# Attention units between projection groups, 128-row token transposes and a split output projection in an encoder block

## The chip, the cores and the metric

The kernel runs on one core of one Trainium2 chip. The metric is the device time of one launch in microseconds (us), lower is better. A core has TensorE (PE; its weight loads are listed apart as PEld), VectorE (DVE), ScalarE (ACT), GpSimd (POOL) and SyncE (SP), which run their own instruction streams and wait for each other on semaphores; 16 DMA engines move data.

## What is computed

One layer of a bidirectional encoder on a prompt of 1024 tokens and a sample of 512, all in float32, 1024 channels. The core of the reference:

```python
xn = rmsnorm(x, norm1_g[l])
proj = xn @ w_in[l]                       # q, k, v: 3 groups x 4 heads x 64 each; u: 768
for g, (win, dil) in enumerate(GROUPS):   # ((128, 1), (512, 4), (2048, 16))
    o, lse = dilated_group(q[:, :, g], k[:, :, g], v[:, :, g], ..., dil, (win // 2) // dil)
...
att = jnp.sum(wts[..., None] * jnp.stack(outs, axis=0), axis=0)
four = fourier_mix(u)
gates = jax.nn.sigmoid((xn @ w_gate[l] + b_gate[l]).astype(jnp.float32))
...
mix = gates[:, :, 0] * (att @ w_attn_br[l]) + gates[:, :, 1] * (four @ w_four_br[l])
x = x + mix @ w_out[l]
x = x + expert_choice(rmsnorm(x, norm2_g[l]), w_router[l], w_exp_gate[l], w_exp_up[l], w_exp_down[l])
```

Each query of a head group sees 64 keys to either side in its residue class of the dilation (1, 4 or 16). The expert choice picks, for each of 16 experts, the 128 prompt tokens and 64 sample tokens with the highest router weight, and runs a SwiGLU with 2048 inner channels on them.

## The kernel before

Matrix products of float32 values are mostly done as three products of the fast float32r type: an operand is split into a rounded high part (ACT copies it) and a low part (DVE subtracts), and high x high, high x low and low x high are summed in PSUM. Products that aren't split run as plain float32. The program is a chain of blocks with a barrier between; in a block each engine has an order written by hand.

**Norm.** RMSNorm, transposes of the tokens to xhigh and xlow, and the bias tables. Ends near 67 us.

**Projections and attention** (lines 466 to 775). For each head group g, `project(g)` on PE makes q and k with 12 groups of 24 matmuls of 512 columns (lines 603 to 605), then v with 12 groups of 24 matmuls of 256 columns (lines 572 to 574). PSUM banks 6 and 7 take turns; ACT copies q out, DVE k and v. The values go through DRAM to be put in order by residue class: SP stores the 12 token tiles (`vrows<-vst`, 8 slots), waits until all are stored, and loads 12 to 16 tiles `V` (`class_rows`). Then come the 12 attention units of the group, a unit being 128 queries of one class with its 4 heads: `scores(n)` on PE (line 623), `biased(n)` on DVE (line 722: adds the bias, takes the maximum), `exps(n)` on ACT (line 678), `turn(n)` on PE (transposes, line 639), `turned(n)` on ACT and DVE (copies to pT), `outputs(n)` on PE (line 655) and the copy to `orow` on DVE (line 743). PE's order is scores(n), turn(n-2), outputs(n-3). After the third group, `channels()` makes u: 36 groups of 24 matmuls of 256 columns. Weight block n of w_in lies in one of two buffers, is loaded when block n-2 is done, and cut in two by `high_block` (ACT, 2048 columns) and `low_block` (DVE).

Units come in three kinds. Of the 36, 16 have one piece of 128 keys (the sample of group 1, all of group 2); 20 have two pieces. Of those, 8 have two pieces of 128 keys, and 12 one of 128 and one of 64 (all 8 prompt units of group 1, and the first and last of each sequence in group 0, where the residue class begins or ends).

**Fourier mixing and merge**, then **gates** (three-part products); not touched.

**Router** (from 1267 us). For each of 12 token tiles PE runs `out(t)` (line 1185): mix @ w_out as 16 plain float32 matmuls of 512 columns, then `turn` (line 1195: 8 transposes), `logits` (1205) and `turn_aff` (1212) of earlier tiles. DVE adds the residual, norms and makes the softmax. Once the 8 prompt tiles have their logits, DVE also searches the top 128 of 1024 tokens in 16 rounds (`top(0, r)`), and after the last tile the top 64 of 512 in 8 rounds. SP loads the first expert's units 0, 1 and 2 of weights (2 MB each) into `raw` at the start of this block.

**Experts** (from 1518 us, lines 1389 to 1600). A loop over 16 experts. POOL gathers the chosen rows (`xg`), PE transposes them in `turn_tokens` (lines 1446 and 1447: 8 times 128 rows of the prompt and 64 rows of the sample, by turns), ACT and DVE split them, and PE runs `gate_up` and `down` while ACT and DVE split the streamed weights. `turn_tokens(e + 1)` stands behind the second of eight steps of `down(e)`.

```python
                for g in range(NG):
                    project(g)
                    a, b = first_unit[g], first_unit[g + 1]
                    for n in range(a, b + 3):
                        if n < b:
                            scores(n)
                        if a <= n - 2 < b:
                            turn(n - 2)
                        if a <= n - 3:
                            outputs(n - 3)
                channels()
```

## Time and profile before

| | us |
|---|---|
| median of 3 runs | 3399.98 |
| the three runs | 3392.88, 3399.98, 3400.17 |
| profiled execution | 3397.87 |
| its span in the trace | 3395.8 |
| busy in the span: PE / PEld | 3189.2 / 2761.7 |
| busy: DVE / ACT / POOL | 1855.9 / 1435.8 / 119.2 |

The span is the time from the first to the last instruction of the profiled execution; the rest lies around it. The granted clock is TensorE's: 1.00 is 2.4 GHz, 0.50 is 1.2 GHz. A matmul's duration in a row is longer than its share of a stream, since matmuls overlap; what one costs in a stream is the distance between starts.

### The profile page before, as it was taken

The numbers are of one execution on the slowest core, as the hardware profiler recorded it, in microseconds if no ns is written. First come the engines' busy times: TensorE is split into PE (matmuls) and PEld (weight loads), VectorE is DVE, ScalarE is ACT, GpSimd is POOL, SyncE is SP. The second block draws the span as 40 slices with busy tenths as digits, with TensorE's granted clock in tenths as the row PEclk, the third lists the DMA queues.
The fourth block names the chain that finished last, engine by engine and source line by source line (L and its number), as shares of the span: only waits on it lengthen the run. The fifth ranks groups of instructions, "written<-read, shape, count | busy, mean of one in ns | idle before, by whom it ended". The sixth has DMA issues, their size and how long they took to land. (4 is left out here: it accounts for less than half of the span.)

```text
span 3395.8 us, 45550 instructions
## 1 busy us (share of the span) xinstructions
PE 3189.2 (94%) x17512; PEld 2761.7 (81%) x17512; DVE 1855.9 (55%) x2764; ACT 1435.8 (42%) x1969; POOL 119.2 (4%) x133
## 2 busy tenths in 40 slices
PE   5989898999999999949999999999999999999993
PEld 4878787974778774529999999999999999999993
DVE  4141313042443422486777777777777777767773
ACT  4030312121432322225555655565556555655552
POOL 0000000000000000000000000000000000000000
PEclk9989696999999999969999999999999999999997
DMA  4111111031233334226766777677667766777664
GB/s 165 41 57 39 55 35 63 17 102 44 77 91 95 110 118 167 75 81 210 238 229 233 249 238 228 229 247 238 228 234 249 237 228 235 248 231 228 234 229 164
DMA packets 468127, 553.25 MB, mean 163 GB/s; under 512 B 14379, under 2 KB 384043, under 8 KB 467916
## 3 DMA queue, kind: packets, MB, share of 16 engines
q1 hardware_dynamic: 460876, 526.94, 45.8%
q0 software_dynamic: 7168, 25.17, 3.3%
q8 instruction: 56, 0.92, 0.1%
q14 instruction: 27, 0.22, 0.0%
HBM read 507.87 MB, written 44.19 MB: 163 GB/s over the span
## 5 line engine op out<-in xcount | busy, mean ns | idle before, releaser
L1462 PE MATMUL ps<-xsplit,wh 128*128 128x384 f32 x4096 | 1167.8, 359 | 2.2 <-DVE xsplit L1557 2.2
L1464 PE MATMUL ps<-xsplit,wl 128*128 128x192 f32 x4096 | 1026.2, 251 | 0.0
L1550 DVE TENSOR_TENSOR wl<-raw,wh 128x2048 fp32r<-128x2048 f32 x384 | 876.9, 2284 | 115.0 <-ACT wh L1507 113.9
L1507 ACT ACTIVATE wh<-raw 128x2048 fp32r<-128x2048 f32 x384 | 734.5, 1914 | 347.5 <-PE ps L1486 321.7
L1464 PEld LDWEIGHTS ps<-xsplit,wl 128*128 128x128 f32 x4096 | 783.3, 191 | 0.6
L1462 PEld LDWEIGHTS ps<-xsplit,wh 128*128 128x128 f32 x4096 | 769.6, 188 | 3.0 <-issue 2.4
L1521 ACT ACTIVATE low<-ps 128x384 f32<-128x384 f32 x256 | 126.0, 492 | 433.4 <-PE ps L1464 433.4
L1566 DVE TENSOR_TENSOR gu<-ps,low 128x384 f32<-128x384 f32 x256 | 142.8, 558 | 219.9 <-ACT low L1521 219.9
L1079 DVE TENSOR_TENSOR glow<-graw,ghigh 128x1024 fp32r<-128x1024 f32 x72 | 88.1, 1225 | 237.3 <-ACT ghigh L1035 237.3
L1481 PE MATMUL ps<-wh,hsplit 128*128 128x512 f32 x512 | 201.9, 394 | 0.0
L1483 PE MATMUL ps<-wl,hsplit 128*128 128x512 f32 x512 | 200.4, 391 | 0.0
L1485 PE MATMUL ps<-wh,hsplit 128*128 128x512 f32 x512 | 200.4, 391 | 0.0
L1486 PE MATMUL ps<-wl,hsplit 128*128 128x512 f32 x512 | 200.1, 391 | 0.0
L1482 PE MATMUL ps<-wh,hsplit 128*128 128x512 f32 x512 | 200.1, 391 | 0.0
L1035 ACT ACTIVATE ghigh<-graw 128x1024 fp32r<-128x1024 f32 x72 | 76.4, 1061 | 213.4 <-DMA graw<-in_w_gate_dram 138.8
L572 PE MATMUL ps<-whigh,xhigh 128*128 128x256 f32 x576 | 164.3, 285 | 2.0 <-ACT u L709 1.4
L1020 PE MATMUL ps<-xh,ghigh 128*128 128x512 f32 x384 | 152.6, 397 | 13.1 <-DVE xlow L1086 13.1
L573 PE MATMUL ps<-wlow,xhigh 128*128 128x256 f32 x576 | 164.0, 285 | 0.0
L574 PE MATMUL ps<-whigh,xlow 128*128 128x256 f32 x576 | 163.9, 285 | 0.0
L1021 PE MATMUL ps<-xlow,ghigh 128*128 128x512 f32 x384 | 152.0, 396 | 0.0
L1022 PE MATMUL ps<-xh,glow 128*128 128x512 f32 x384 | 151.8, 395 | 0.0
L678 ACT ACTIVATE sc<-sc,negm 128x128 f32<-128x128 f32 (+2 forms) x144 | 61.9, 432 | 171.1 <-DVE negm L728 171.1
(205 smaller groups left out, 4484.6 us busy)
## 6 DMA issues: line engine op xcount, KB each, us to landing
raw<-in_w_exp_gate_dram SPq DMA_DIRECT2D x128, 1024.0 KB, 5.2
raw<-in_w_exp_up_dram SPq DMA_DIRECT2D x128, 1024.0 KB, 7.4
raw<-in_w_exp_down_dram SPq DMA_DIRECT2D x128, 1024.0 KB, 6.1
graw<-in_w_gate_dram SPq DMA_DIRECT2D x96, 256.0 KB, 2.8
wraw<-in_w_in_dram SPq DMA_DIRECT2D x12, 1024.0 KB, 5.2
graw<-in_w_four_br_dram SPq DMA_DIRECT2D x24, 384.0 KB, 3.5
xin<-in_x_dram SPq DMA_DIRECT2D x12, 512.0 KB, 3.7
xres<-in_x_dram SPq DMA_DIRECT2D x12, 512.0 KB, 3.5
```

Source lines behind the costliest of these rows:

```text
L572: pe.matmul(bank, high[k], whigh[:, n % 2, k, :], start=k == 0, stop=False)
L573: pe.matmul(bank, high[k], wlow[:, n % 2, k, :], start=False, stop=False)
L574: mm = pe.matmul(bank, low[k], whigh[:, n % 2, k, :], start=False, stop=k == KT - 1)
L1462: pe.matmul(ps[:, bank, 0:2 * CAP], wh[:, q % AHEAD, tile], xsplit[:, k, :, :].rearrange("p s t -> p (s t)"), start=k == 0, stop=False)
L1464: mm = pe.matmul(ps[:, bank, CAP:2 * CAP], wl[:, q % AHEAD, tile], xsplit[:, k, 0, :], start=False, stop=k == KT - 1)
L1481: pe.matmul(prompt, hsplit[:, k, H_LOW], wh[:, q % AHEAD, cols], start=first, stop=False)
L1482: pe.matmul(prompt, hsplit[:, k, H_HIGH], wh[:, q % AHEAD, cols], start=False, stop=False)
L1483: pe.matmul(prompt, hsplit[:, k, H_HIGH], wl[:, q % AHEAD, cols], start=False, stop=end)
L1485: pe.matmul(sample, hsplit[:, k, H_SAMPLE], wh[:, q % AHEAD, cols], start=first, stop=False)
L1486: mm = pe.matmul(sample, hsplit[:, k, H_SAMPLE], wl[:, q % AHEAD, cols], start=False, stop=end)
L1507: act.activation(cut_part(wh, q), raw_part(q), ACT.Copy).then_inc(w_high, 1)
L1550: dve.tensor_tensor(cut_part(wl, q), raw_part(q), cut_part(wh, q).bitcast(F32), ALU.subtract).then_inc(w_cut, 1)
```

## The change

Four things.

1. **Order of projections and attention.** The two sequences get their own q, k and V tiles (P for prompt, S for sample). Groups of matmuls run in the order v, q, k of the prompt, then v, q, k of the sample, for each head group, then u. The units of one part (head group, sequence) run during the groups of the next part: behind a group of matmuls PE runs outputs(n-2), turn(n-1), scores(n). A part of 8 units meets 8 groups (4 of v, 2 of q, 2 of k) and starts one unit behind each; a part of 4 units starts one behind every second group. Scores have 2 PSUM banks in place of 4, sc 2 buffers in place of 3. The weight blocks are now 18 of the same 256 columns for q, k and v (9 before), each loaded for either sequence, and 3 for u.
2. **Values.** Stores of v tiles and loads of V are issued by POOL in place of SP, with 3 slots in place of 8, and each part's loads stand between its own v and q groups.
3. **Output projection.** `out(t)` runs 48 float32r matmuls (lines 1239 to 1241 of the changed kernel) in place of 16 plain float32. ACT and DVE first split w_out (16 pieces of 128x512 each) and then each tile of the mix, one tile ahead. The split copy of w_out lies where `raw` units 1 and 2 were, so these are loaded behind the last output projection.
4. **Token transposes.** xgS has 128 rows, the last 64 set to zero once by POOL ahead of the first gather; both transposes of a pair now have 128 rows and columns.

PE behind a group of values, in the attention of head group 0, prompt (kT and kP are keys, V and vP values, sc the scores). Before:

```order
L623 MATMUL ps<-kT,qT 128x256 x4
L639 MATMUL ps<-ident,sc 128x128 x8
L655 MATMUL ps<-V,pT 128x64 x8
L623 MATMUL ps<-kT,qT 128x256 x4
L639 MATMUL ps<-ident,sc 128x128 x8
```

Now, at the end of the sample's fourth v group and the start of its first q group (L642 to L644 are v, L628 to L630 are q):

```order
L642 MATMUL ps<-whigh,xhigh 128x256
L643 MATMUL ps<-wlow,xhigh 128x256
L644 MATMUL ps<-whigh,xlow 128x256
L689 MATMUL ps<-vP,pT 128x64 x8
L674 MATMUL ps<-ident,sc 128x128 x8
L658 MATMUL ps<-kP,qP 128x256 x4
L628 MATMUL ps<-xhigh,whigh 128x512
L629 MATMUL ps<-xlow,whigh 128x512
```

The units stood back to back; now 24 matmuls of a projection stand between two of them.

DVE at the start of the router block. Before, behind the last mix of the gates:

```order
L1270 TENSOR_TENSOR xres<-xres,ps 128x512 x2
L1274 TENSOR_SCALAR stat<-stat 128x1
L1276 RECIPROCAL stat<-stat 128x1
```

Now:

```order
L1336 TENSOR_TENSOR xlow<-mix_93,xlow 128x8x128
L1343 TENSOR_TENSOR flow<-fourT,wo_h 128x512 x6
L1343 TENSOR_TENSOR alow<-attT,wo_h 128x512 x2
L1343 TENSOR_TENSOR flow<-fourT,wo_h 128x512 x6
L1343 TENSOR_TENSOR alow<-attT,wo_h 128x512 x2
L1336 TENSOR_TENSOR xlow<-mix_93,xlow 128x8x128
L1355 TENSOR_TENSOR xres<-xres,ps 128x512 x2
```

DVE's first residual add now stands behind one split of the mix, 16 of w_out and the next of the mix.

The diff, cut to its core:

```diff
-        qT = at("qT", 128, [P, 2, TOKENS])
-        kT = at("kT", 140, [P, 2, TOKENS])
-        V = at("V", 152, [P, MAXV, GW])
-        band = at("band", 168, [P, 2 * HEADS, 2 * P])
-        same = at("same", 176, [P, 2, HEADS, P])
-        sc = at("sc", 180, [P, 3, HEADS, 2 * P])
+        VSLOTS = 3
+        qT = [at("qP", 128, [P, 2, SEQS[0][1]]), at("qS", 164, [P, 2, SEQS[1][1]])]
+        kT = [at("kP", 136, [P, 2, SEQS[0][1]]), at("kS", 168, [P, 2, SEQS[1][1]])]
+        V = [at("vP", 144, [P, MAXV[0], GW]), at("vS", 172, [P, MAXV[1], GW])]
+        band = at("band", 156, [P, 2 * HEADS, 2 * P])
+        same = at("same", 177, [P, 2, HEADS, P])
+        sc = at("sc", 181, [P, 2, HEADS, 2 * P])
+        vst = at("vst", 189, [P, VSLOTS, GW])
...
+        wo_h = at("wo_h", 96, [P, KT, D], F32R)
...
-        xg = [at("xgP", 88, [CAPS[0], D]), at("xgS", 92, [CAPS[1], D])]
-        raw = [at(f"raw{i}", kb, [P, 16, WB]) for i, kb in enumerate((96, 112, 176, 128))]
+        xg = [at("xgP", 88, [P, D]), at("xgS", 92, [P, D])]
+        raw = [at(f"raw{i}", kb, [P, 16, WB]) for i, kb in enumerate((176, 96, 112, 128))]
...
+        for g in range(NG):
+            for s, (base, size) in enumerate(SEQS):
+                first = len(groups)
+                for kind in "vqk":
+                    n = len(block_groups)
+                    block_groups.append([])
+                    for i in range(size // P if kind == "v" else 2 * size // CH):
+                        block_groups[n].append(len(groups))
+                        groups.append(Group(kind, n, g, s, i % 2 if kind != "v" else i, i // 2))
+                phases.append((first, len(groups)))
...
+        starts = [[] for _ in groups]
+        n = 0
+        for (g, s), (first, end) in zip([(g, s) for g in range(NG) for s in range(2)], phases[1:]):
+            count = sum((x[0], x[2].s) == (g, s) for x in units)
+            for j in range(count):
+                starts[first + j * min(2, (end - first) // count)].append(n)
+                n += 1
...
+        def cut_after(n):
+
+            return block_groups[n - 1][min(1, len(block_groups[n - 1]) - 1) if len(block_groups[n - 1]) > 2 else 0]
+
+        cut_at = {cut_after(n): n for n in range(2, NB)}
...
+            @block.gpsimd
+            def _(pool):
+                def class_rows(g, s):
+                    base, size = SEQS[s]
+                    if g:
+                        pool.wait_ge(o_ev, units_before(g - 1, s))
+                    rows_of = vrows[base:base + size, :]
+                    first = sum(x[0] < s for x in PLANS[g][1])
+                    for v, (_, r, classes, a) in enumerate([x for x in PLANS[g][1] if x[0] == s]):
+                        rows = rows_of.rearrange("(n r) f -> r n f", r=GROUPS[g][1] // classes)
+                        pool.dma_start(v_tile(s, g, first + v), rows[r, a:a + P, :]).then_inc(v_ld, 16)
+
+                for p, x in enumerate(groups):
+                    if x.kind != "v":
+                        continue
+                    if x.i == 0 and x.n:
+                        pool.wait_ge(v_ld, v_loads(*((x.g, 0) if x.s else (x.g - 1, 1))))
+                    slot, before = v_slot(p)
+                    pool.wait_ge(*evacuated(p))
+                    row = SEQS[x.s][0] + x.i * P
+                    pool.dma_start(vrows[row:row + P, :], vst[:, slot, :]).then_inc(v_st[slot], 16)
+                    if p == block_groups[x.n][-1]:
+                        for q in block_groups[x.n][-VSLOTS:]:
+                            slot, before = v_slot(q)
+                            pool.wait_ge(v_st[slot], 16 * (before + 1))
+                        class_rows(x.g, x.s)
...
-                for g in range(NG):
-                    project(g)
-                    a, b = first_unit[g], first_unit[g + 1]
-                    for n in range(a, b + 3):
-                        if n < b:
-                            scores(n)
-                        if a <= n - 2 < b:
-                            turn(n - 2)
-                        if a <= n - 3:
-                            outputs(n - 3)
-                channels()
+                for p, x in enumerate(groups):
+                    project(p, x)
+                    for n in starts[p]:
+                        if n >= 2:
+                            outputs(n - 2)
+                        if n >= 1:
+                            turn(n - 1)
+                        scores(n)
+                outputs(NU - 2)
+                turn(NU - 1)
+                outputs(NU - 1)
...
+                dve.wait_ge(t_out, 16)
+                for p, x in enumerate(groups):
+                    if p:
+                        for n in starts[p - 1]:
+                            if n == 0:
+                                dve.wait_ge(t_tab, 16 * 3)
                             biased(n)
-                        if a <= n - 2 < b:
-                            turned(n - 2)
-                        if a <= n - 3:
-                            outputs(n - 3)
-                        if n == a + 2:
-                            low_block(dve, 3 * g + 4)
-                low_block(dve, 11)
+                    if x.kind in "kv":
+                        evacuate(p, x)
+                    if p in cut_at:
+                        low_block(dve, cut_at[p])
+                    for n in starts[p]:
+                        if n >= 2:
+                            outputs(n - 2)
+                        if n >= 1:
+                            turned(n - 1)
+                outputs(NU - 2)
+                turned(NU - 1)
+                outputs(NU - 1)
...
+                sp.wait_ge(r_y, 2 * NT)
+                for j in (1, 2):
+                    load_unit(sp, 0, j)
...
+                    high, low = mix_part(t, 0), mix_part(t, 1)
                     for nb in range(2):
+                        bank, cols = ps[:, 6 * (t % 2) + nb, :], slice(nb * CH, (nb + 1) * CH)
                         for k in range(KT):
-                            mm = pe.matmul(ps[:, 6 * (t % 2) + nb, :], mix_of(t // 4)[:, k, (t % 4) * P:(t % 4 + 1) * P],
-                                           w_out_at(k)[:, nb * CH:(nb + 1) * CH], start=k == 0, stop=k == KT - 1)
+                            if t == 0:
+                                pe.wait_ge(wo_cut, nb * KT + k + 1)
+                            pe.matmul(bank, high[:, k, :], wo_h[:, k, cols], start=k == 0, stop=False)
+                            pe.matmul(bank, high[:, k, :], w_out_low(k)[:, cols], start=False, stop=False)
+                            mm = pe.matmul(bank, low[:, k, :], wo_h[:, k, cols], start=False, stop=k == KT - 1)
                         mm.then_inc(r_y, 1)
...
+                high_mix(0)
+                high_w_out()
...
+                def low_mix(t):
+                    dve.wait_ge(mix_high, t + 1)
+                    dve.tensor_tensor(mix_part(t, 1), mix_tile(t), mix_part(t, 0).bitcast(F32), ALU.subtract).then_inc(mix_cut, 1)
+
+                def low_w_out():
+                    for nb in range(2):
+                        for k in range(KT):
+                            cols = slice(nb * CH, (nb + 1) * CH)
+                            dve.wait_ge(wo_high, nb * KT + k + 1)
+                            dve.tensor_tensor(w_out_low(k)[:, cols], w_out_at(k)[:, cols], wo_h[:, k, cols].bitcast(F32),
+                                              ALU.subtract).then_inc(wo_cut, 1)
+
+                low_mix(0)
+                low_w_out()
...
+                pool.memset(xg[1][CAPS[1]:P, :], 0.0).then_inc(x_zero, 1)
+                pool.wait_ge(x_zero, 1)
...
-                        at_col = (k % 2) * CAP
-                        pe.transpose(ps[:, k // 2, at_col:at_col + CAPS[0]], xg[0][:, k * P:(k + 1) * P], ident[:, :])
-                        mm = pe.transpose(ps[:, k // 2, at_col + CAPS[0]:at_col + CAP], xg[1][:, k * P:(k + 1) * P],
-                                          ident[0:CAPS[1], 0:CAPS[1]])
+                        at_col = (k % 2) * 2 * P
+                        pe.transpose(ps[:, k // 2, at_col:at_col + P], xg[0][:, k * P:(k + 1) * P], ident[:, :])
+                        mm = pe.transpose(ps[:, k // 2, at_col + P:at_col + 2 * P], xg[1][:, k * P:(k + 1) * P], ident[:, :])
```

## Rows read from the trace of the kernel before

**Rows 1.** Windows: length; busy (count) of PE, PEld, DVE, ACT, POOL; clock; DMA; GB/s.

```profile
69.50:704.30 634.80, 593.79 (x3552) 531.24 (x3552) 133.98 (x502) 124.52 (x395) 0.00 (x0) 0.87 0.14 44
173.00:242.20 69.20, 56.92 (x384) 48.40 (x384) 34.22 (x147) 31.99 (x111) 0.00 (x0) 0.83 0.21 66
344.50:432.40 87.90, 76.81 (x336) 63.60 (x336) 30.78 (x149) 28.67 (x113) 0.00 (x0) 0.60 0.18 55
535.40:596.30 60.90, 46.68 (x240) 42.42 (x240) 25.73 (x145) 25.05 (x109) 0.00 (x0) 0.54 0.22 70
1267.30:1420.40 153.10, 147.74 (x489) 77.86 (x490) 36.93 (x84) 36.96 (x65) 0.00 (x0) 0.98 0.41 144
1420.40:1518.00 97.60, 59.68 (x201) 34.10 (x200) 88.97 (x158) 14.96 (x30) 0.17 (x2) 0.74 0.10 38
```

**Rows 2.** Timeline of PE, projections: start us, us, engine, line, operation, count.

```profile
86.54 0.39 PE L605 MATMUL ps<-xhigh,wlow 128*128 128x512 f32 x1
...
137.76 0.28 PE L572 MATMUL ps<-whigh,xhigh 128*128 128x256 f32 x1
...
157.08 0.28 PE L574 MATMUL ps<-whigh,xlow 128*128 128x256 f32 x1
```

**Rows 3.** Timeline of PE, two units of head group 0.

```profile
221.82 1.90 PE L655 MATMUL ps<-V,pT 128*128 128x64 f32 x16
223.65 1.13 PE L623 MATMUL ps<-kT,qT 64*128 64x256 f32 x8
225.22 1.03 PE L639 MATMUL ps<-ident,sc 128*64 128x128 f32 x8 [0.44 <-issue]
226.09 2.76 PE L655 MATMUL ps<-V,pT 128*128 128x64 f32 x15
...
228.81 0.49 PE L623 MATMUL ps<-kT,qT 64*128 64x192 f32 x3
```

**Rows 4.** Timeline of PE, head group 2, scores of two following units.

```profile
568.75 1.33 PE L623 MATMUL ps<-kT,qT 64*128 64x128 f32 x8
...
572.65 0.61 PE L623 MATMUL ps<-kT,qT 64*128 64x128 f32 x2
```

**Rows 5.** A window inside the attention of head group 0.

```profile
205.00:240.00 35.00, 33.45 (x271) 29.81 (x269) 20.51 (x91) 18.52 (x66) 0.00 (x0) 1.00 0.09 33
```

**Rows 6.** Timeline of PE, first matmuls behind two gaps.

```profile
185.68 1.94 PE L639 MATMUL ps<-ident,sc 128*128 128x128 f32 x8 [6.05 <-DVE pT L509]
...
857.94 0.77 PE L1020 MATMUL ps<-xh,ghigh 128*128 128x512 f32 x1 [4.60 <-DVE xlow L1086]
```

**Rows 7.** Timeline of the first unit: DVE's first bias, PE's first transposes.

```profile
174.13 0.36 DVE L722 CUSTOM_DVE_ANT_0 sc<-ps,band 128x192 f32<-128x192 f32 x1 [1.19 <-PE ps L623]
...
177.49 1.07 PE L639 MATMUL ps<-ident,sc 128*64 128x128 f32 x8 [0.97 <-ACT sc L678]
```

**Rows 8.** Timeline of PE, one row of the router block.

```profile
1377.90 5.31 PE L1185 MATMUL ps<-fourT,xnT 128*128 128x512 f32 x12
...
1391.64 1.04 PE L1195 MATMUL ps<-ident,xn 128*128 128x128 f32 x8
...
1394.33 1.88 PE L1185 MATMUL ps<-fourT,xnT 128*128 128x512 f32 x4
```

**Rows 9.** Groups by line and form: busy us, mean ns, idle before.

```profile
L1086 DVE TENSOR_TENSOR xlow<-xnT,xh 128x1024 fp32r<-128x1024 f32 x12 | 13.9, 1219 | 0.0
```

**Rows 10.** Timeline of PE, token transposes of an expert in the loop.

```profile
1620.71 0.33 PE L1446 MATMUL ps<-ident,xgP 128*128 128x128 f32 x1
...
1621.17 0.33 PE L1446 MATMUL ps<-ident,xgP 128*128 128x128 f32 x1
```

**Rows 11.** The page's costliest group.

```profile
L1462 PE MATMUL ps<-xsplit,wh 128*128 128x384 f32 x4096 | 1167.8, 359 | 2.2 <-DVE xsplit L1557 2.2
```

**Rows 12.** Timeline of POOL and PE at the start of the experts.

```profile
1520.48 2.38 POOL L1419 DMA_INDIRECT xgS<-normed,idx_inS  x1 [0.30 <-issue]
...
1528.10 0.48 PE L1446 MATMUL ps<-ident,xgP 128*128 128x128 f32 x1 [11.16 <-DMA xgS<-normed,idx_inS]
```

More of the change, by code:

```diff
@@ L475, in encoder @@
         v_st, v_ld = sems("v_st", VSLOTS), sem("v_ld")
[L477 to L483 removed]
         units = [(g, i, t) for g in range(NG) for i, t in enumerate(PLANS[g][0])]
[L486 to L487 removed]
+        NU = len(units)
@@ L489, in encoder @@
         u_tiles = [(s, par, j) for s, (_, n) in enumerate(SEQS) for par in range(2) for j in range(n // 2 // P)]
-        first_unit = [next(n for n, v in enumerate(units) if v[0] == g) for g in range(NG)] + [len(units)]
-        NU = len(units)
+        Group = namedtuple("Group", "kind n g s i c")
+        groups, block_groups, phases = [], [], []
+        for g in range(NG):
[8 more added lines that the diff above has]
+                phases.append((first, len(groups)))
@@ new lines, in encoder @@
+        for m in range(3):
+            n = len(block_groups)
+            block_groups.append(list(range(len(groups), len(groups) + NT)))
+            groups += [Group("u", n, None, None, i, m) for i in range(NT)]
+        phases.append((block_groups[-3][0], len(groups)))
+        NB = len(block_groups)
+        starts = [[] for _ in groups]
[5 more added lines that the diff above has]
+                n += 1
@@ new lines, in evacuated, with units_before, v_loads @@
+        def evacuated(p):
+            kinds = {"q": "q", "k": "kv", "v": "kv", "u": "u"}
+            kind = kinds[groups[p].kind]
+            return {"q": q_ev, "kv": kv_ev, "u": u_ev}[kind], sum(kinds[x.kind] == kind for x in groups[:p + 1])
+        def units_before(g, s):
+            return sum((u[0], u[2].s) <= (g, s) for u in units)
+        def v_loads(g, s):
+            return 16 * sum(1 for h in range(NG) for v in PLANS[h][1] if (h, v[0]) <= (g, s))
+        v_groups = [p for p, x in enumerate(groups) if x.kind == "v"]
@@ L616, in scores @@
                 def scores(n):
                     g, i, t = units[n]
-                    if n >= 2:
-                        pe.wait_ge(s_max, 4 * (n - 1))
+                    if n == 0 or units[n - 1][0] != g or units[n - 1][2].s != t.s:
+                        for kind, sem_ in (("q", q_ev), ("k", kv_ev)):
+                            last = max(p for p, x in enumerate(groups) if (x.kind, x.g, x.s) == (kind, g, t.s))
+                            pe.wait_ge(sem_, evacuated(last)[1])
+                    if n:
+                        pe.wait_ge(s_max, 4 * n)
@@ L711, in _ @@
+                for p, x in enumerate(groups):
+                    if p:
+                        for n in starts[p - 1]:
+                            exps(n)
+                    if x.kind in "qu":
+                        evacuate(p, x)
+                    if p in cut_at:
+                        high_block(act, cut_at[p])
+                    for n in starts[p]:
+                        if n >= 1:
+                            turned(n - 1)
+                turned(NU - 1)
             @block.vector
```

277 lines of the change are left out of this document (121 added, 156 removed).

## The prediction

> **What bounds the kernel now.** I read the page first: PE is busy for nearly all of the span, in the expert loop without a break (its costliest group waited 2.2 us in all [rows 11]). So time can be won only where PE waits, where it runs at half clock, or where its own work shrinks. Next the windows by stage [rows 1]. Projections and attention take 634.8 us at a mean granted clock of 0.87. The loss lies in the three attention stretches of 69.2, 87.9 and 60.9 us, at clocks of 0.83, 0.60 and 0.54: PE looks busy there, but much of it at 1.2 GHz. In the router PE is busy for 147.7 of the first 153.1 us, then DVE takes over with 89.0 of 97.6 us.
>
> Then the timeline of PE, to see why the clock falls. PE stands still for 6 us until the values have come back from DRAM and the turned scores can be copied [rows 6], and the attention behind that gap runs at half pace. In head group 0 it recovers: for 35 us units run at 1.00 with PE busy for 33.45 us [rows 5]. In groups 1 and 2 it hardly does.
>
> **1. Projections and attention.** I build the new stage as a sum of PE's work at full clock, since every other engine has less to do.
>
> Projections: 864 matmuls of 512 columns. From 86.54 to 137.76 us 226 of them start, so one costs 0.227 us: 195.8 us. Then 1728 of 256 columns; 161 start between 137.76 and 157.08 us, 0.120 each: 207.4 us [rows 2]. Splitting by sequence changes no count. Together 403.2 us.
>
> Units: two pieces of 128 keys: outputs 1.83 (221.82 to 223.65), scores 1.13 (to 225.22, less 0.44 idle), transposes 0.87 (to 226.09), 3.83 us. With a 64-key piece the outputs take 2.72 (226.09 to 228.81), so 4.72 us [rows 3]. With one piece I have only the half-clock row: 3.90 us from scores to scores [rows 4], so 1.95 us at full clock. Sum: 8 x 3.83 + 12 x 4.72 + 16 x 1.95 = 118.5 us.
>
> Is the new order fed? The tightest steps are v groups with a unit behind each (12 of them, 4 in each sample part). PE's work in one is 24 x 0.120 = 2.88 us plus the unit, 6.7 us for two full pieces. Beside it runs the chain from scores(n) to turn(n). The first unit shows it: DVE's first bias at 174.13, PE's transposes at 177.49, 3.4 us for 192 keys [rows 7]. I add 1.2 us for the scores ahead of the bias (DVE's wait in that row), an estimated 0.6 us for 256 keys in place of 192 and 0.9 us for the transposes themselves: 6.1 us. It just fits. One-piece units have 4.8 us of PE work, and a chain shorter in proportion. Behind q and k groups (24 x 0.227 = 5.4 us more) there is room. In each sample part's v block, DVE has a weight cut in the same queue ahead of the orow and pT copies and the next bias, so the next bias comes some 2 us late; PE then waits 1.5 us, three times: 4.5 us. Elsewhere cuts hide behind q and k groups. Small gaps: rows 3 shows one of 0.44 us; between 0 and 0.44 x 36 = 16 us, I take 4, since the projection group in between absorbs most. The first matmuls still run slow, 3 us as before. At the end outputs(34), turn(35) and outputs(35) stand behind the last u group, and the block can't end before the last copy and store: 3 us more than the short tail now. Sum: 403.2 + 118.5 + 4.5 + 4 + 3 + 3 = 536.2 us against 634.8. **Gain 98.6 us**, bounds 85 and 112. Where it comes from: about 45 us of standing still, the rest clock.
>
> Values: the stall of 6 us goes because the loads of a part now have its q and k groups as cover (8 x 5.4 = 43 us in a prompt part). Now POOL issues them. No row shows a plain DMA from POOL; its dearest indirect one takes 2.38 us [rows 12], so 12 loads take 29 us at most, under the cover. For stores, 3 slots give 3 x 2.88 = 8.6 us from copy to reuse in the first part, against some 2.4 us to issue and a few to land. I cost it at nothing. SP's attrows stores now stand among weight loads; three orow buffers cover that.
>
> **2. Token transposes.** A pair in the loop costs 1621.17 - 1620.71 = 0.46 us, 3.68 us for 8 [rows 10]. Eight transposes of 128 rows in one shape take 1.04 us as a row, ending beside the next start [rows 8]; less the overlap of the last, 0.11 us each. So 16 equal ones take 1.76 us: 1.92 us less. PE never waits in the loop [rows 11], so all of it counts: 15 x 1.92 = 28.8 us, and about 1.9 us for the first expert. The sample's now move 128 columns where 64 were moved. Upper bound of the cost: a second one as dear as the first, 0.26 us (0.46 less the other's 0.20), so 4.2 us and a loss of 0.5 us each; I take the equal-shape row since it is the same form of instruction. **Gain 30.7 us**, bounds -8 and 31.
>
> Here the Trainium skill speaks against the change: "TensorE: Matmul & The Clock Gate", section "Why this matters for your kernels", says that a small-K matmul takes the same time as a full one. By that rule no time hides in the 64-row shape, and more columns can only add. The trace says otherwise for a mix: 0.23 us on average against 0.11.
>
> **3. Output projection.** A row of the router takes 1394.33 - 1377.90 = 16.43 us, of it 13.74 for 16 plain products, 0.86 each; 48 split ones take 48 x 0.227 = 10.9 us [rows 2, 8]. That is 2.86 us less per tile. For tiles 2 to 8 PE sets the pace, 7 x 2.86 = 20.0 us; DVE is busy for 36.9 of 153 us there [rows 1], so one more split per tile, 1.22 us [rows 9], hides. Tiles 0 and 1 win 5.7 us but PE starts late: one split of the mix on ACT and on DVE (1024 columns, 1.22 us on DVE [rows 9], a little less on ACT) and the first piece of w_out (512 columns, half of that) go first. By my estimate PE starts some 3.1 us later than now, and has then stood still for 5 us. Behind a gap of 4.60 us its matmuls take 0.77 us for 0.39 [rows 6, 2], which costs another 3 us. DVE's 16 pieces, at 0.61 us or a little more each, keep up with PE's 3 x 0.227 = 0.68. Net 0.4 us lost. From tile 9 on DVE sets the end, with two more splits in its queue (tiles 10 and 11): 2.4 us. **Gain 17.2 us**, bounds 8 and 24. The 4 MB of weights that are now loaded behind the last product have over 40 us of top-k search as cover.
>
> **4. The memset** of 64x1024 on POOL stands ahead of the first gather, for which PE waits 11.16 us [rows 12]. Between nothing and twice a DVE pass over 1024 columns (1.22 us [rows 9]); I take 1.2 us lost.
>
> **Sum.** 98.6 + 30.7 + 17.2 - 1.2 = 145.3 us off the profiled execution of 3397.87 us, which lies 2.1 us below the median. From the median 3399.98: **3255 us**.
>
> **Rivals.**
> *Half clock in the tight steps.* The bubbles and transposes of the twelve v steps let the clock drop there. For it: attention ran long stretches at 0.5 with PE busy. Against: rows 5, and in each step now some 3 us of the dense matmuls behind which the clock recovered each time. All twelve (6.7, 7.6 and 4.8 us in the three parts) cost 4 x 19.1 = 76 us more: 3331; half of them 3293. The same page of the Trainium skill, "Part 4: PE-mode transpose", says that transposes don't count as work for the clock; this speaks for the rival, rows 5 against it.
> *Transposes as dear as now.* Only the row count matters, not the mix: the 30.7 us go, up to 8 more are lost: 3286 to 3294.
> *POOL's queue throttles values.* If a store takes over 8.6 us from copy to landing, v groups wait for slots. At 12 us each dense group takes 4 instead of 2.88; over the 24 prompt groups that is 27 us: 3282. The Trainium skill, "SBUF — State Buffer", section "SBUF: two separate sides", says that a POOL-issued DMA takes about 3.1 us in place of 0.62 while a DVE copy of two-port kind holds the shared port; that alone would stay under 8.6 us.
> *Slower than before.* The clock stays at 0.5 through the interleaved stretch, as it did for most of head groups 1 and 2, with PE busy [rows 1]. From the end of the first part PE has 466 us of work at full clock; a share s of it at half clock adds 466 x s, which eats all 145 us from s = 0.31. At s = 0.5 it is 3488.
> *The order doesn't bite:* units wait on their chain as now, at full clock. Then each of 12 tight steps loses some 3 us: 3291.
>
> **How the numbers follow.** Forecast 0.58 (3233 to 3275); half clock in tight steps 0.13; transposes 0.11; POOL 0.06; chain 0.05; persistent half clock 0.04; the rest on the fast side 0.03. The range 3233 to 3305 holds the forecast, most of the transpose, POOL and chain cases and the lighter half of the first rival, some 0.83. What a measurement can tell from no change is about 0.2% (7 us); only the persistent half clock reaches that: faster 0.95, same 0.01, slower 0.04.
>
> **What would show it.** In the changed profile: clock near 1.00 from 76 us to the end of u; that stage 536 us long; no gap of PE over 2 us inside; pairs of token transposes at 0.22 us; router rows at 13.6 us and DVE still last there; POOL's stores spaced by the v groups, not by themselves. A stage over 560 us, or windows at 0.5 in the v blocks, would show the first step wrong; a pair at 0.46 us or more the second.

## The result, and where the 131.7 us went

| | before | changed |
|---|---|---|
| median, us | 3399.8 | 3264.9 (3262.0 to 3265.9) |
| ratio to before, 95% interval | | 0.9606 (0.959 to 0.962) |
| span of the profiled execution, us | 3395.8 | 3264.1 |

The forecast was 3255 us, its range 3233 to 3305. The sum by stage comes from the first matmul of each stage. First the timeline of PE before (start, us, line, what; in brackets the idle time ahead), then after:

```profile
711.21 6.73 PE L814 MATMUL ps<-tabS,u 128*128 128x256 f32 x16 [7.03 <-DMA chan_sb<-c_chan_dram]
1267.41 2.81 PE L1185 MATMUL ps<-fourT,mix 128*128 128x512 f32 x6 [1.85 <-PEq L975]
...
3343.51 0.39 PE L1486 MATMUL ps<-wl,hsplit 128*128 128x512 f32 x1
```

```profile
630.15 5.53 PE L850 MATMUL ps<-tabS,u 128*128 128x256 f32 x16 [8.77 <-DMA chan_sb<-c_chan_dram]
1187.43 0.77 PE L1239 MATMUL ps<-wo_h,xlow 128*128 128x512 f32 x1 [4.89 <-DVE flow L1343]
1430.79 0.45 PE L1535 MATMUL ps<-ident,xgP 128*128 128x128 f32 x1 [13.85 <-DMA xgS<-normed,idx_inS]
3212.12 0.39 PE L1574 MATMUL ps<-wl,hsplit 128*128 128x512 f32 x1
```

With 1528.10 us for the first token transposes of before [rows 12]:

| stage | before | after | change | forecast |
|---|---|---|---|---|
| to the first Fourier matmul | 711.21 | 630.15 | -81.1 | -98.6 |
| from there to the first output projection | 556.20 | 557.28 | +1.1 | (+3.1, start of the split) |
| from there to the first token transposes | 260.69 | 243.36 | -17.3 | -19.1 |
| from there to the last matmul | 1815.41 | 1781.33 | -34.1 | -30.7 |
| tail | 52.3 | 52.0 | -0.3 | 0 |

The forecast of rows 2 and 3 together is -17.2 for the projection and +1.2 for the memset, -16.0; they gave -16.2, of which 2.0 belong to Fourier mixing and gates (557.28 less 3.04 of later start, against 556.20), so the two terms themselves gave -14.2. The windows of the changed kernel (length; busy and count of PE, PEld, DVE, ACT, POOL; clock; DMA; GB/s) answer [rows 1]:

```profile
69.40:621.40 552.00, 549.42 (x3552) 489.44 (x3552) 154.03 (x510) 143.92 (x404) 42.42 (x78) 0.99 0.20 67
180.00:300.00 120.00, 120.00 (x752) 104.18 (x751) 41.67 (x122) 32.78 (x84) 11.88 (x22) 1.00 0.23 76
300.00:470.00 170.00, 168.86 (x992) 145.13 (x991) 55.08 (x197) 46.03 (x141) 14.06 (x26) 0.96 0.21 69
470.00:621.40 151.40, 150.82 (x1148) 143.27 (x1146) 28.24 (x116) 40.60 (x123) 2.17 (x4) 1.00 0.13 42
```

The stage of projections and attention took 634.8 us with 593.8 busy at 0.87. Now it takes 552.0 with 549.4 busy at 0.99. Both halves of the reasoning are seen: PE doesn't wait, and it isn't slow. Still the stage is 16 us longer than the 536.2 of the forecast. The unit rows show why. One-piece unit of head group 2, followed by the first matmul of a group; then outputs, transposes and scores of a unit of head group 1 with pieces of 128 and 64 keys:

```profile
501.02 1.00 PE L689 MATMUL ps<-vP,pT 128*128 128x64 f32 x8
501.85 0.61 PE L674 MATMUL ps<-ident,sc 128*128 128x128 f32 x4
502.39 1.32 PE L658 MATMUL ps<-kP,qP 64*128 64x128 f32 x8
503.64 0.39 PE L642 MATMUL ps<-whigh,xhigh 128*128 128x256 f32 x1
...
311.89 2.87 PE L689 MATMUL ps<-vP,pT 128*128 128x64 f32 x16
314.69 1.07 PE L674 MATMUL ps<-ident,sc 128*64 128x128 f32 x8
315.69 1.75 PE L658 MATMUL ps<-kP,qP 64*128 64x192 f32 x8
317.36 0.50 PE L628 MATMUL ps<-xhigh,whigh 128*128 128x512 f32 x1
```

The unit takes 503.64 - 501.02 = 2.62 us where the sum had 1.95. Outputs and transposes did get short with the clock, 0.83 and 0.54 us. The scores did not: 1.25 us from 502.39 to 503.64 at full clock. Before, at half clock, they took as much, from the row of 568.75 [rows 4] to this row of the kernel before:

```profile
570.01 1.11 PE L639 MATMUL ps<-ident,sc 128*128 128x128 f32 x4
```

That is 1.26 us. So the scores don't scale with the clock here. The scores of head groups 1 and 2 read every 4th or 8th column of qT and kT (`class_cols`); those of head group 0 read neighbouring ones. That became the main question for the chip.

POOL, whose price for a plain DMA no row of before showed, was cheap (line, form, count; busy us, mean ns; idle before):

```profile
L608 POOL DMA_DIRECT2D vrows<-vst x36 | 19.7, 548 | 403.7 <-DVE vst L789 403.7
```

A plain DMA takes POOL 0.55 us to issue, and DVE never waits for a slot: ahead of its copies to vst it waits for PE alone. Now the router and the experts, tile to tile and transpose to transpose:

```profile
1240.22 0.47 PE L1239 MATMUL ps<-wo_h,xlow 128*128 128x512 f32 x1
...
1253.84 0.48 PE L1239 MATMUL ps<-wo_h,xlow 128*128 128x512 f32 x1
...
1521.50 0.27 PE L1535 MATMUL ps<-ident,xgP 128*128 128x128 f32 x1
1521.61 0.27 PE L1536 MATMUL ps<-ident,xgS 128*128 128x128 f32 x1
```

A router row takes 13.62 us (16.43 before [rows 8]), a pair of transposes 2 x 0.11 (0.46 before [rows 10]).

### The profile page after: what moved, and what is told of

Its sections match the earlier page's. It is cut to its first block and busy times, and to the rows that moved or that the text cites. A ratio compares the mean times of both kernels' runs of the same rounds, so it can differ in the third digit from the quotient of the medians.

```text
span 3264.1 us, 46120 instructions
## 1 busy us (share of the span) xinstructions
PE 3080.3 (94%) x17704; PEld 2751.0 (84%) x17704; DVE 1898.6 (58%) x2801; ACT 1471.7 (45%) x2006; POOL 164.2 (5%) x212
## 5 line engine op out<-in xcount | busy, mean ns | idle before, releaser
L642 PE MATMUL ps<-whigh,xhigh 128*128 128x256 f32 x576 | 168.1, 292 | 2.6 <-PEq L318 2.6
L644 PE MATMUL ps<-whigh,xlow 128*128 128x256 f32 x576 | 164.8, 286 | 0.0
L1056 PE MATMUL ps<-xh,ghigh 128*128 128x512 f32 x384 | 151.8, 395 | 13.5 <-DVE xlow L1122 13.5
L642 PEld LDWEIGHTS ps<-whigh,xhigh 128*128 128x128 f32 x576 | 113.6, 197 | 9.9 <-issue 9.8
```

The source lines that it names most:

```text
L642: pe.matmul(bank, high, whigh[:, w, k, :], start=k == 0, stop=False)
L644: mm = pe.matmul(bank, low, whigh[:, w, k, :], start=False, stop=k == KT - 1)
```

## Experiments

Each edits the changed kernel (3264.9 us) unless said otherwise. They ran in several sessions, and the kernel before gave medians of 3397.9 to 3399.8 us in them, so differences of under 2 us say nothing.

**1. Is it the order, or the early values?** Kernel before, values first; units still back to back:

```diff
-            return (n % 3) * ATT_W + (n // 3) * WB if n < 9 else 3 * ATT_W + (n - 9) * WB
+            return (2, 0, 1)[n % 3] * ATT_W + (n // 3) * WB if n < 9 else 3 * ATT_W + (n - 9) * WB
...
+                    pe.wait_ge(b_cut, 3 * g + 1)
+                    for i in range(NT):
+                        bank_free(g, p)
+                        tokens_first(p, 3 * g, [[x[:, k, i * P:(i + 1) * P] for k in range(KT)] for x in (xhigh, xlow)])
+                        p += 1
                     for b in range(2):
-                        n = 3 * g + b
+                        n = 3 * g + 1 + b
```

> The kernel before with one edit: in each head group the values are projected first, then q, then k, so that their trip through DRAM lies behind 12 groups of 512-column matmuls. The units still stand back to back behind the projections of their group. Theory A (the stall ahead of the units is what drops the clock, and the clock is what makes the units slow): the three attention stretches run near full clock, some 150 us in place of the 218 us of before, so about 3400 - 68 = 3332 us. Theory B (units need dense matmuls between them to be fed and clocked): only the three stalls of 6 us go, and the clock still falls in the units of head groups 1 and 2: 3400 - 18 = 3382 us. If it lies between, the windows by stage tell which head group kept its clock.

Measured: 3376.3 us against 3398.0 of before on the same chip, ratio 0.993 (0.9915 to 0.995). Windows over most of the attention of head groups 1 and 2:

```profile
345.00:425.00 80.00, 76.46 (x332) 63.84 (x333) 29.41 (x141) 28.42 (x113) 0.00 (x0) 0.57 0.07 23
524.00:588.00 64.00, 56.47 (x310) 51.89 (x309) 26.40 (x146) 25.56 (x111) 0.00 (x0) 0.60 0.13 43
```

Theory B holds: no wait of PE in the attention is over 3.2 us now, where each head group had one of 6 us, and the clock fell all the same, 0.57 and 0.60 with PE busy for 88 to 96% of the time. (Head group 0 ran at 0.81, before at 0.83.) The 6 us stall wasn't what kept head groups 1 and 2 slow. Units back to back can run at 1.00 too, for 35 us in [rows 5]; what decides between the two isn't shown.

**2. Units back to back in the changed kernel**, values early, all else kept:

```diff
+        steps = []
+        for at, (first, end) in enumerate(phases):
+            steps += [(p, []) for p in range(first, end)]
+            steps += [(None, [m]) for m, v in enumerate(units) if at < 2 * NG and (v[0], v[2].s) == (at // 2, at % 2)]
...
-                for p, x in enumerate(groups):
-                    project(p, x)
-                    for n in starts[p]:
+                for p, ns in steps:
+                    if p is not None:
+                        project(p, groups[p])
+                    for n in ns:
```

> The changed kernel with one edit: the units of a part stand back to back behind the groups of their own part, none between the groups of the next part. The early values, the six parts, the two score banks and all else stay. Theory (the groups between the units cover the chain scores, bias, exp, transposes): a unit takes its chain of about 6 us with two pieces and 4.5 with one, 20 x 6 + 16 x 4.5 = 192 us in place of about 135 of work, and the clock may fall on top: 55 to 80 us more, 3320 to 3345 us. Rival (the values in time were all of the gain): 0 to 15 us more, at most 3280 us.

Measured: 3348.6 us, 84 more; the first Fourier matmul is at 714.43 us, 84.3 later, and 3 later than before the change. Two groups of PE and the windows over three stretches with units, one of each head group:

```profile
L681 PE MATMUL ps<-ident,sc 128*128 128x128 f32 x200 | 49.4, 391 | 23.5 <-ACT sc L720 23.3
...
L681 PE MATMUL ps<-ident,sc 128*64 128x128 f32 x24 | 9.4, 397 | 5.3 <-ACT sc L720 5.3
```

```profile
140.00:200.00 60.00, 51.24 (x241) 42.05 (x242) 20.44 (x92) 21.01 (x73) 0.00 (x0) 0.60 0.09 32
330.00:395.00 65.00, 62.96 (x317) 52.88 (x317) 22.08 (x92) 19.51 (x70) 2.17 (x4) 0.67 0.07 24
500.00:545.00 45.00, 35.96 (x181) 29.89 (x181) 16.98 (x97) 14.76 (x65) 0.00 (x0) 0.60 0.14 48
```

PE waits for the exponentials for 28.8 us in all. In the changed kernel the first of the two groups waits 1.5 in place of 23.5:

```profile
L674 PE MATMUL ps<-ident,sc 128*128 128x128 f32 x200 | 31.1, 279 | 1.5 <-ACT sc L712 1.5
```

The rest, some 55 us, is clock: 0.60 to 0.67 in these stretches where it was 0.96 to 1.00. The groups between the units do both jobs, and in the changed kernel the whole gain of this stage hangs on them. One thing stands against reading this as the price of back-to-back order in general: the changed kernel has 2 banks for scores and turns each unit one step sooner than the kernel before, so its units, once back to back, wait on their chain more. With the old order kept, early values did win something (experiment 1: the first Fourier matmul at 694.81 us, 16.4 sooner).

**3. Token transposes.** First the shapes undone, `xg[1][0:CAPS[1], ...]` and a 64x64 identity, by turns with the 128-row ones (the memset stays):

> The changed kernel with one part undone: each pair of token transposes is again one of 128 rows and one of 64 rows, by turns. The memset stays. Theory (the alternation or the 64-row shape made a pair dear): a pair goes from 0.218 back to 0.46 us, 15 x 8 x 0.24 = 29 us more and some 2 us for the first expert: 3264.9 + 31 = 3296 us. Rival (in this kernel the pair is short because other code round it changed): within 5 us of 3265.

Measured: 3299.9 us, 35 more. Then 64-row transposes, but four of one kind behind four of the other:

```diff
-                    for k in range(KT):
...
+                    for half in range(2):
+                        for k in range(4 * half, 4 * half + 4):
+                            at_col = (k % 2) * 2 * P
+                            pe.transpose(ps[:, k // 2, at_col:at_col + P], xg[0][:, k * P:(k + 1) * P], ident[:, :])
+                        for k in range(4 * half, 4 * half + 4):
+                            at_col = (k % 2) * 2 * P
+                            mm = pe.transpose(ps[:, k // 2, at_col + P:at_col + CAP], xg[1][0:CAPS[1], k * P:(k + 1) * P],
+                                              ident[0:CAPS[1], 0:CAPS[1]])
+                        mm.then_inc(x_T, 1)
```

> The changed kernel with 64-row sample transposes, but not by turns: in each half of turn_tokens four 128-row transposes of the prompt come first, then four of 64 rows. Theory (what costs is each change from one row count to the other): only 4 changes per expert instead of 16, so most of the 31 us stays won: 3265 + 8 = 3273 us at most. Rival (a transpose of 64 rows is dear by itself, in any order): as with all of it undone, some 3296 to 3300 us.

Measured: 3267.2 us, 2.3 more. Timelines, first by turns, then grouped:

```profile
1636.14 0.27 PE L1536 MATMUL ps<-ident,xgS 64*128 64x64 f32 x1
1636.34 0.33 PE L1535 MATMUL ps<-ident,xgP 128*128 128x128 f32 x1
1636.60 0.27 PE L1536 MATMUL ps<-ident,xgS 64*128 64x64 f32 x1
```

```profile
1630.37 0.60 PE L1536 MATMUL ps<-ident,xgP 128*128 128x128 f32 x4
1630.90 0.46 PE L1539 MATMUL ps<-ident,xgS 64*128 64x64 f32 x4
1631.29 0.66 PE L1536 MATMUL ps<-ident,xgP 128*128 128x128 f32 x4
```

By turns a pair costs 0.46 us, two changes of row count in it; grouped, eight transposes cost 0.92 us with two changes in all. From start to start, the trace of the grouped kernel has 0.11 us for a transpose of 128 rows behind its like and 0.06 for one of 64 rows and columns. So the 64-row shape is not dear, it is the cheaper one, and what cost is the change of row count between neighbours: (0.46 - 0.11 - 0.06) / 2 = some 0.145 us for each. The Trainium skill, "TensorEngine Tiling (Array Packing)", section "Key Properties", states that changing the tiling mode drains TensorE. The runs agree that a change costs; that it is a drain they don't show.

**4. Output projection undone:**

```diff
-                            pe.matmul(bank, high[:, k, :], wo_h[:, k, cols], start=k == 0, stop=False)
-                            pe.matmul(bank, high[:, k, :], w_out_low(k)[:, cols], start=False, stop=False)
-                            mm = pe.matmul(bank, low[:, k, :], wo_h[:, k, cols], start=False, stop=k == KT - 1)
+                            mm = pe.matmul(bank, mix_tile(t)[:, k, :], w_out_at(k)[:, cols], start=k == 0, stop=k == KT - 1)
```

> The changed kernel with the output projection undone: 16 plain float32 matmuls per tile, no splits of w_out and of the mix. The late load of the expert weights stays. Theory (the term of the sum): rows of the router go from 13.6 back to 16.4 us and the start comes some 3 us earlier, 17 us in all: 3265 + 17 = 3282 us. Rival (DVE's chain set the router's end anyway): under 5 us more.

Measured: 3281.8 us, 16.9 more. The term of 17.2 us stands, and the rival of under 5 us is out.

**5. Strided scores.** q and k are written by class:

```diff
-                        act.activation(qT[x.s][:, x.i, x.c * CH:(x.c + 1) * CH], ps[:, 6 + p % 2, :], ACT.Copy,
+                        act.activation(by_class(qT[x.s][:, x.i, :], x), bank_by_class(p, x), ACT.Copy,
...
+        def by_class(view, x):
+
+            w = CH // STEP[x.g, x.s]
+            return view.rearrange("p (r n) -> p r n", r=STEP[x.g, x.s])[:, :, x.c * w:(x.c + 1) * w]
```

> The changed kernel with one edit: ACT and DVE write q and k by residue class when they copy them out of PSUM, so that the scores of head groups 1 and 2 read 128 to 192 neighbouring columns, not every 4th or 8th. Theory (it is the stride of the scores' operands that made them cost at full clock what they cost at half): a one-piece unit takes 1.95 in place of 2.62 us, 16 x 0.67 = 10.7, and the 8 prompt units of head group 1 some 0.5 us less each: 15 us off, 3250 us, unless the copies get dearer. Rival (64-row operands or waits make them slow): no change, 3265 us.

Measured: 3249.8 us, 15.1 less; the first Fourier matmul is at 614.90 us, 15.25 sooner. The same unit as above:

```profile
488.88 1.00 PE L703 MATMUL ps<-vP,pT 128*128 128x64 f32 x8
489.72 0.61 PE L688 MATMUL ps<-ident,sc 128*128 128x128 f32 x4
490.26 0.71 PE L672 MATMUL ps<-kP,qP 64*128 64x128 f32 x8
490.90 0.39 PE L656 MATMUL ps<-whigh,xhigh 128*128 128x256 f32 x1
```

Scores take 0.64 us in place of 1.25, the unit 2.02. The copies out of PSUM, which now read every 4th or 8th element, cost ACT 598 ns and DVE 691 for 512 columns, as before.

Which operand is it? Only q (the stationary one), then only k (the moving one):

> The changed kernel with only q written by residue class; k stays in token order, so that the scores of head groups 1 and 2 have a contiguous stationary operand (q, which the weight load reads) and a strided moving one (k). Theory A (the strided weight load is the dear one: the rows of its weight loads shrank from 275 to 200 ns with both in class order, and the excess per matmul is alike for 128 and 192 moving columns): all of the 15 us, 3250 us, scores of 64x128 at some 0.30 us. Theory B (the strided moving read is the dear one): nothing gained, 3265 us, scores at 0.46 us.

> The changed kernel with only k written by residue class: the stationary operand q is strided, the moving one k is contiguous. With only q in class order 4.5 us were won of 15.2. Theory (both strides cost, the moving one more, and they add up): 15.2 - 4.5 = some 10 us off, 3255 us, the scores' weight loads at 275 ns as in the changed kernel and scores of 64x128 at some 0.33 us. Rival (either stride alone keeps the scores dear, and only both together free them): again some 4 us off, 3260 us.

Measured: 3260.4 and 3256.9 us, 4.5 and 8.0 less; their first Fourier matmuls are at 624.41 and 620.73 us, 5.7 and 9.4 sooner. The mean of a one-piece score in the rows by form (line of the scores, 64x128, 64 of them) was 462 ns in the changed kernel, 424 with q alone, 424 with k alone and 314 with both: each alone saves 38 ns, both together 148. The distances from the first score of a unit to the matmul behind its scores, all at full clock, say the same. First q alone, then k alone, one-piece units:

```profile
497.23 1.18 PE L672 MATMUL ps<-kP,qP 64*128 64x128 f32 x8
498.34 0.39 PE L656 MATMUL ps<-whigh,xhigh 128*128 128x256 f32 x1
```

```profile
493.63 1.22 PE L672 MATMUL ps<-kP,qP 64*128 64x128 f32 x8
494.78 0.39 PE L656 MATMUL ps<-whigh,xhigh 128*128 128x256 f32 x1
```

| scores of a prompt unit, us | both strided | q in class order | k in class order | both in class order |
|---|---|---|---|---|
| one piece, 128 keys | 1.25 | 1.11 | 1.15 | 0.64 |
| two pieces, 192 keys | 1.67 | 1.54 | 1.19 | 0.85 |

So each stride has its price, and the two do not add up. For 128 keys either stride alone keeps the scores dear (0.47 or 0.51 us above 0.64, both 0.61), as the rival of the second run had it. For 192 keys the moving one (k) is the dearer: alone it costs 0.69 us, the stationary one 0.34, both 0.82. By these rows q alone saves 16 x 0.14 + 8 x 0.13 = 3.3 us and k alone 16 x 0.10 + 8 x 0.48 = 5.4, not 15. That 5.7 and 9.4 make 15.1 is chance: the stage of projections and attention had 13.7 us at half clock in the changed kernel, 10.2 with both in class order, 6.8 with q alone and 3.4 with k alone. Theory A and theory B of the first run are both false.

**6. A better version.** On top of class order, the memset moved ahead and the last outputs drained early:

```diff
+            @block.gpsimd
+            def _(pool):
+                pool.wait_ge(r_y, 2 * NT)
+                pool.memset(xg[1][CAPS[1]:P, :], 0.0).then_inc(x_zero, 1)
...
+                    if p == LAST + 2:
+                        outputs(NU - 2)
+                        turn(NU - 1)
+                    if p == LAST + 4:
+                        outputs(NU - 1)
```

> The version with q and k written by residue class, and two edits more: the memset of xgS stands in the router block behind the last output projection, and the outputs of the last two units stand behind the second and fourth u group after the last scores, not behind all of u. Theory: the first token transposes come 2.3 us sooner after the router, and Fourier mixing starts some 1.9 us sooner since no store of rows is left to wait for: 3249.75 - 4.2 = 3245.5 us. Rival for the first: the memset was not on the path, 0. Rival for the second: the loads and the barrier at the start of Fourier mixing set its start, 0.

Measured: 3242.2 us. The first Fourier and token rows:

```profile
609.97 0.79 PE L871 MATMUL ps<-tabS,u 128*128 128x256 f32 x1 [6.81 <-DMA chan_sb<-c_chan_dram]
...
1408.02 0.45 PE L1561 MATMUL ps<-ident,xgP 128*128 128x128 f32 x1 [11.61 <-DMA xgS<-normed,idx_inS]
```

PE's waits fell from 8.6 to 6.8 us and from 13.5 to 11.6 (class order alone had 8.61 and 13.51), 3.7 us for the 4.2 expected. The median fell by 7.6. The first stage also had 6.8 us at half clock in place of 10.2, worth up to 1.7. Not all of the rest is traced: four kernels with the same first stage (the changed one, 3 and 4) have their first Fourier matmul between 628.63 and 630.26 us, so a part is scatter.

Last, what experiment 3 taught, put to the units with pieces of 128 and 64 keys. The four heads share a PSUM bank, and now all of them are open at once, so only the first matmul has the start flag. (The Trainium skill, "PSUM — Partial Sum Buffer", section "Terms": it clears the written bits of the whole bank, and a matmul without it overwrites where they are clear. No run here tests it apart.)

```diff
-                    for h in range(HEADS):
-                        for c, (v, w, p0) in enumerate(t.keys):
+                    for c, (v, w, p0) in enumerate(t.keys):
+                        for h in range(HEADS):
...
+                                           v_tile(t.s, g, v)[p0:p0 + w, h * HD:(h + 1) * HD], start=c == 0 and h == 0, stop=c == len(t.keys) - 1 and h == HEADS - 1)
```

> The version with class order, early memset and early drain (3242.15 us), and one edit more: outputs runs the first key piece of all four heads, then the second piece of all four; the first matmul alone has the start flag. In the 12 units with a piece of 128 and one of 64 keys the row counts no longer alternate. Theory (alternating row counts cost, as the token transposes showed): their outputs go from 2.80 to some 1.9 us, 12 x 0.9 = 11 us off: 3231 us. Rival (it is the 64-row operand itself, or small matmuls cost alike in any order): 3242 us, within 2.

Measured: 3232.9 us, ratio 0.951 (0.9496 to 0.9525) to before; the first Fourier matmul is at 599.94 us, 10.0 sooner. The unit that took 2.80 us for its outputs:

```profile
305.31 2.03 PE L705 MATMUL ps<-vP,pT 128*128 128x64 f32 x16
307.27 1.06 PE L690 MATMUL ps<-ident,sc 128*64 128x128 f32 x8
308.27 0.92 PE L674 MATMUL ps<-kP,qP 64*128 64x192 f32 x8
309.12 0.50 PE L644 MATMUL ps<-xhigh,whigh 128*128 128x512 f32 x1
```

Outputs take 307.27 - 305.31 = 1.96 us, scores 309.12 - 308.27 = 0.85 (they were 2.80 and 1.67). Six changes of row count fewer, 0.84 us less: 0.14 for each, as in the transposes. Inside a group, matmuls of 64 and of 128 rows stand alike, 0.11 us apart, so the theory holds and the rival (the 64-row operand itself) is out. This version beats the changed kernel by 32 us.

## Why the prediction was right, and where not

**Projections and attention: right mechanism, one term mis-sized.** 98.6 us forecast, 81.1 measured. The term is "16 x 1.95" for one-piece units, made by halving the 3.90 us of a unit at half clock. Of those, the scores' 1.26 us don't halve: measured 2.62, 16 x 0.67 = 10.7 us. The same error sits in the 8 prompt units of head group 1, costed like those of group 0 with 1.13 us for the scores: they take 317.36 - 315.69 = 1.67 us, 8 x 0.54 = 4.3. Together 15.0 us, where 17.5 are missing, and experiment 5, which takes the strides away, gives 15.25 back.

Could the trace of before have told? Rows 4 could not: at half clock the stride hardly shows. Scores of 192 keys at half clock took 299.30 - 297.71 = 1.59 us in class order (experiment 5) and 1.67 strided; it is at full clock that the one falls to 0.85 and the other stays. But the trace of before has strided scores at full clock, ahead of the stall of head group 2, a row and a window over it:

```profile
535.49 2.28 PE L623 MATMUL ps<-kT,qT 64*128 64x128 f32 x16 [0.56 <-issue]
```

```profile
535.50:538.00 2.50, 2.32 (x18) 2.04 (x18) 1.01 (x9) 0.00 (x0) 0.00 (x0) 1.00 0.15 52
```

That is 0.14 us for each of 16 at full clock, close to what one costs at half clock (1.26 / 8 = 0.16). By this row the scores of a one-piece unit come to some 1.14 us and not to 0.63. The Trainium skill speaks of it, in "SBUF — State Buffer", section "Door 1: The DMA port swizzle (why `[64,N]` ≈ `[32,N]`)": accesses get full bandwidth where at least two fall in one 16-byte line. With every 4th or 8th float32 each access is a line of its own. The runs agree: 0.16 us in place of 0.08 at those strides, nothing lost at every 2nd (of the stationary operand, the last section has the figures).

**Stalls and clock.** The 4.5 us behind weight cuts and 4 us of small gaps were too dear: PE stood still for 552.0 - 549.4 = 2.6 us in the stage. The clock took it back: four short stretches, from 306.2, 336.9, 381.3 and 463.2 us on, ran at 0.50, 13.7 us in all, which costs up to half of that, 6.8 us. Two of them:

```profile
306.20:309.60 3.40, 3.40 (x17) 2.56 (x16) 1.65 (x8) 0.55 (x1) 0.00 (x0) 0.50 0.11 40
463.20:466.60 3.40, 3.40 (x19) 3.18 (x18) 1.31 (x10) 1.06 (x5) 0.00 (x0) 0.50 0.02 5
```

That is the first rival, at under a tenth of its 76 us. Ahead of the last of the four PE had waited 1.14 us for ACT, ahead of the others it had not waited at all. What brings on such a stretch wasn't tried. So the stage's forecast was helped by errors of opposite sign: 15.0 us of strides and up to 6.8 of clock too little, 5.9 of waits too much; some 1.6 us stay untraced. The split of the gain was off a little as well: the prediction puts some 45 us to standing still, [rows 1] have 634.8 - 593.8 = 41.0 and 2.6 of them are left.

**Why rival "slower" did not come.** Its danger was real: experiments 1 and 2 show units back to back at 0.57 to 0.67 in head groups 1 and 2, and at 0.60 and 0.81 in head group 0. With a dense group between two units the granted clock stays at 0.96 to 1.00. The prediction's evidence for this was weaker than it took it to be: [rows 5] show 1.00 for 35 us without such groups, and the same order ran at 0.60 elsewhere.

**Token transposes.** 30.7 forecast, 34.1 measured (35 by experiment 3). Equal shapes at 0.11 us each was right, the rival is ruled out. Grouping alone would have given nearly all, with no memset and no wider transposes. Most of the 3.4 us above the forecast is clock, which the sum didn't have. Before, an expert of the loop took 112.9 us from its transposes to the next one's, and 114.5 in two of them, where the clock fell to 0.50 some 4 us behind the start of the transposes by turns. One of the two, behind transposes from 2184.3 us on:

```profile
2188.50:2191.90 3.40, 3.40 (x9) 2.62 (x9) 2.92 (x3) 0.45 (x2) 0.00 (x0) 0.50 0.14 50
```

The changed kernel has no such stretch in the loop, the kernel of experiment 3 by turns has three. That is 2 x 1.6 = 3.2 us.

**Output projection.** 17.2 forecast, 16.9 by experiment 4. PE's start came 4.89 - 1.85 = 3.04 us later (3.1 forecast).

**Memset.** 1.2 forecast; the wait for the first tokens grew from 11.16 to 13.85 us, 2.7. The memset itself is short, 0.95 us; what else of the wait belongs to it, only moving it ahead in experiment 6 shows (back to 11.61, and 11.64 in the last version; kernels with the memset in its old place wait 13.3 to 15.4):

```profile
1417.83 0.95 POOL L1518 MEMSET xgS<- 64x1024 f32 x1 [940.96 <-POOLq L1206]
```

**Not in the sum:** the 2.0 us that Fourier mixing and gates took less. In all: 145.3 forecast, 131.7 in the profile, 134.9 in the medians.

## What to carry to other kernels

Small dependent matmuls belong between dense groups of independent ones: this hides their chain and keeps the granted clock, and here neither early data nor a shorter stall did it alone. Before a duration at half clock is halved, compare it with a like operation at full clock: strided scores took the same at both clocks, and a change of row count in the outputs 0.19 us at half clock (experiment 2) and 0.14 at full, not half. And compare a strided operation with a strided one at full clock, if the trace has any. Order small matmuls and transposes so that equal row counts stand together, and write what they read in the order in which it is read.

## What was new about the hardware

- Float32 operands of a matmul read at a stride of 16 or 32 bytes: 64x128 scores take 0.16 us for each of the 8 matmuls of a row (1.25 / 8) in place of 0.08 (0.64 / 8), and 0.16 at 1.2 GHz as at 2.4. At 1.2 GHz the stride costs next to nothing (192 keys: 1.67 against 1.59 us). Stationary and moving stride do not add up: with 128 moving columns either alone costs most of what both cost (0.47 and 0.51 us a unit, 0.61). As stationary operand at 8 bytes (u, whose tokens are read by parity) nothing is lost beside 256 moving columns of float32r, 0.12 us as for v (in the changed kernel from 614.82 to 614.94 us); a moving operand at 8 bytes wasn't tried.
- ACT and DVE copying 512 columns out of PSUM at the same strides: no change (598 and 691 ns).
- Matmuls of 128 and 64 rows by turns: 0.14 to 0.15 us for each change at full clock, in the outputs (7 changes in a unit against 1, 2.80 against 1.96 us) and in transposes.
